# A two-block transformer kernel on one core: the start of the first FFN rebuilt, and three small jobs moved into the first mixer

## The chip, the cores and the metric

One Trainium2 chip (trn2), one NeuronCore of it. The metric is device time in microseconds (us) of one execution of the whole kernel, from its first instruction to its last and what lies around them; lower is better. A NeuronCore has five engines with queues of their own: TensorE (PE, matmuls, with weight loads shown as PEld), VectorE (DVE), ScalarE (ACT), GpSimd (POOL) and SyncE (SP, which issues the loads).

## The reference

Two transformer blocks on 256 tokens of width 1024, in float32. What matters here, cut from it:

```python
def first_block(x, ...):                       # 256 tokens x 1024
    h = h + 0.5 * swiglu(rmsnorm(h, ffn1_norm), ffn1_w_gate, ffn1_w_up, ffn1_w_down)   # FFN, hidden 2816
    n = rmsnorm(h, mix_norm); z = n @ w_in                                             # first mixer:
    ...  # attention, a spatial gate whose 8 weights of 128x128 (gmlp_w_s) are lower triangular
    h = h + merged @ w_out
    h = h + 0.5 * swiglu(rmsnorm(h, ffn2_norm), ffn2_w_gate, ffn2_w_up, ffn2_w_down)
    return rmsnorm(h, final_norm)

def second_block(x, meta_tokens, lb_logits, ...):
    h = concatenate([meta_tokens, x])          # 16 meta tokens ahead of the 256
    lower_bounds = cumsum(softmax(lb_logits))  # of the forget gates of its recurrent mixer
    ...  # recurrent mixer and latent attention, merged
    h = h + rms_norm((silu(gt) * up) @ w_ffn_out, ffn_post_g)                          # third FFN
```

## The kernel before

**Precision.** Every float32 operand of a projection is split into a high part (rounded to the fast float32 format `F32R`, by ACT: a copy) and a low part (value less high part, by DVE: a subtraction). A product is three matmuls (`products`, L1408 to L1410): high x low, low x high, high x high.

**Slabs.** The weights stream in as slabs of 1 MB (128 x 2048 numbers) through a ring of three (`RING`). For slab n: SP loads `stage`, when slab n-3 is split; ACT writes `w_hi` (`split_hi`, L1062), when PE has used slab n-3; DVE writes `w_lo` (`split_lo`, L1225); PE does 48 matmuls of 256 columns with it. All four engines run a program written out by hand in a fixed order, and wait on each other's semaphores alone.

**FFN.** Eleven pairs J of hidden chunks; each pair takes three slabs: gate, up, down. DVE scales the gate sums by the row factor (L1248), ACT takes the Silu (L1090), DVE scales the up sums (L1256), multiplies (L1260), ACT and DVE split the product (L1099, L1263), and the down slab adds it into PSUM banks 4 to 7 (`down_slab`). Order on PE: gate of J+1, up of J+1, down of J. On DVE and ACT the splits of slabs stand between these steps: split of slab 3, up of J = 0, split of slab 4, gate of J = 1, split of slab 5, up of J = 1, splits of slabs 6 and 7. On all three engines the pairs run in loops of two (`Fori`).

**The first FFN's start.** PE transposes the vectors and x (L1930, L1934) into PSUM. DVE copies x from there to `h` (L1349, `tokens_in`); ACT takes the high part of x times the norm's gain (L1072) and the squares (L1065) from `h`, DVE the low part (L1231). Slab 0 is split in two halves (L1133, L1355), slab 1 in two (L1137, L1374). POOL adds up the squares (L952, L956); PE sums them over the partitions inside slab 1, after 30 of its 48 matmuls (`late_mean`, L1515 to L1518), ACT takes the root (L1081), DVE the inverse (L1238).

**What else stands there.** After slab 1 PE transposes the spatial weights and the meta tokens (L1505, L1509, `spatial_weights_and_meta`). DVE, after the first gate scaling, computes the forget bounds (L1323 to L1326), copies the spatial weights (L1329) and prepares the meta tokens (L1333 to L1340): ten instructions. ACT computes an exponential for the bounds (L1145) with a table load around it. In each FFN ACT clears the banks 4 to 7 by one write of 128 x 2048 zeros (L1108, `y_zeroed`), so that every down matmul can accumulate.

**First mixer.** 26 slabs, written out. DVE evacuates projection i (L427, L431), then splits slab i+3. `scores(0)` on PE stands after projection 4 and uses banks 4 to 7.

Of the kernel before, what the change touches and what calls it, by code (L numbers as in the profile page):

```python
# [20 lines left out]
F32 = mybir.dt.float32  # L21
# [5 lines left out]
P = 128  # L27
# [79 lines left out]
y_bank y_zeroed gate_scaled silu_done up_scaled hidden hid_hi_done hid_lo_done evac  # L107
# [16 lines left out]
def program(nc, a, vec_d, id_d, tab_d, out):  # L124
    ctx = ExitStack()
    with ctx:
# [52 lines left out]
        meta_tok = view(2304, D)  # L179
# [99 lines left out]
        def mixer1_act(act, split_hi, input_hi):  # L279
# [22 lines left out]
            for i in range(26):  # L302
# [13 lines left out]
                if i == 5:  # L316
                    exps(0)
# [27 lines left out]
        def mixer1_dve(dve, split_lo, seq, input_lo, residual, inverse):  # L345
# [3 lines left out]
            def acc(i):  # L349
                k = 6 if i == 2 else 2 * (i % 2)  # L350
                return ps[:, k:k + 2, 0:SEQ]

# [70 lines left out]
            for i in range(26):  # L423
# [47 lines left out]
                if i < 22 and i != 20 or i == 25:  # L471
                    split_lo(n + i + 3)
                if i == 5:
# [466 lines left out]
        def _(pool):  # L940
# [31 lines left out]

            pool.wait_ge(s["ws_T"], 1)
# [5 lines left out]

            pool.wait_ge(s["mean_done"], 1)  # L980
            sum_squares(ssx, sq, "sq_done", 4)
# [51 lines left out]
        def _(act):  # L1033
# [49 lines left out]
            def ffn(f, lookahead=True):  # L1083
# [10 lines left out]
                def hidden(J, m, it=None, pf=True):  # L1094
# [5 lines left out]
                    if pf:  # L1100
# [27 lines left out]
            act.wait_ge(s["vec_ready"], 1)  # L1128
            for b in range(4):
                if b in (0, 2):  # L1130
                    act.wait_ge(s["slab0_in"] if b == 0 else slab_in[0], 16)
                    w = slice(SLAB // 4 * b, SLAB // 4 * b + SLAB // 2)
                    nc.scalar.activation(w_hi[:, 0, w], stage[:, 0, w], ACT.Copy).then_inc(s["hi0_ready" if b == 0 else "hi_ready"], 1)  # L1133
                input_hi(ffn_input(0)[0], vec[:, VEC["ffn1_norm"]:], 0, [b], late=b > 1)
# [65 lines left out]
        def _(dve):  # L1200
# [41 lines left out]
            def ffn(f, rstd_count, lookahead=True):  # L1242
                n, J0 = N_FFN[f], PAIRS * f
                g0 = 0 if f == 0 else 4

                def gate(J, m, it=None, first=False):
                    dve.wait_ge(s["slab_used"], up(m + 1, it))
                    nc.vector.tensor_tensor(pair(ga_s), ps[:, g0:g0 + 2, 0:SEQ] if first else pair(ps[:, J % 2, :]), bc2,  # L1248
# [744 lines left out]
```

## Time and profile before

| | before |
|---|---|
| device time, median of 3 runs | 1068.17 us (1066.13 to 1070.47) |
| the profiled execution | 1068.94 us, its span 1066.8 us |
| PE busy | 1041.7 us, 98% of the span |
| DVE busy | 698.5 us, 65% |
| ACT busy | 518.3 us, 49% |
| POOL busy | 91.1 us, 9% |
| chain that ended last | PE 86%, DVE 7%, ACT 4%, issue 3% |
| granted TensorE clock, mean | 0.990 |

The times in the rows further down count from the span's start; the profiled execution took 2.1 us more than its span. Matmuls are pipelined, so a busy PE says nothing of its pace: the pace is read from the distance of the starts.

### The profile page before, as it was taken

How to read it: one execution, taken by the hardware profiler on the slowest of the kernel's cores; microseconds unless marked ns; L12 is line 12 of the kernel's file. 1: busy time of each engine (PE TensorE's matmuls, PEld its weight loads, DVE VectorE, ACT ScalarE, POOL GpSimd, SP SyncE). 2: the span in 40 equal slices, each digit the busy share in tenths (PEclk: the TensorE clock that was granted, in tenths of full speed). 3: DMA queues.
4: the chain of work that ended last, by engine and by line, in shares of the span. 5: the costliest groups of instructions: out<-in, count | busy, mean ns of one | idle time of the engine just before them, and what ended most of it. 6: DMA issues, size and time to landing. Idle time of an engine off the chain costs nothing.

```text
span 1066.8 us, 20377 instructions
## 1 busy us (share of the span) xinstructions
PE 1041.7 (98%) x8847; PEld 1019.7 (96%) x8847; DVE 698.5 (65%) x705; ACT 518.3 (49%) x572; POOL 91.1 (9%) x90
## 2 busy tenths in 40 slices
PE   8999999999999999999989899999999989999997
PEld 8999999999999999999989798999999989999997
DVE  6765565766958666655689757686747666656652
ACT  6543443636655554444476456513355465444344
POOL 3000000100202200000024800100000030000001
PEclk9999999999999999999999999999999989999999
DMA  9666655465455466566446533333335444665541
GB/s 312 195 210 200 209 175 197 159 207 188 141 175 167 156 213 215 178 199 210 134 135 200 157 119 119 119 100 100 119 119 168 165 143 159 217 207 167 197 156 39
DMA packets 147192, 179.89 MB, mean 169 GB/s; under 512 B 3965, under 2 KB 134258, under 8 KB 147138
## 3 DMA queue, kind: packets, MB, share of 16 engines
q1 hardware_dynamic: 146464, 177.55, 51.3%
q0 software_dynamic: 400, 1.43, 0.4%
q8 instruction: 42, 0.69, 0.3%
q10 hardware_dynamic: 274, 0.13, 0.0%
q14 instruction: 12, 0.10, 0.0%
HBM read 178.05 MB, written 1.05 MB: 168 GB/s over the span
## 4 chain that ended last, share of the span: by engine, by line
PE 86%; DVE 7%; ACT 4%; issue 3%; DMA 1%; DVEq 0%; ACTq 0%; SPq 0%
PE ps L1408 26%; PE ps L1409 26%; PE ps L1410 26%; PE ps L1785 2%; ACT w_hi L1062 2%; DVE w_lo L1225 1%; DMA stage<-in_ffn_w_gate_dram 1%; PE ps L1750 0%; DVE ar L693 0%; ACT L1038 0%; PE ps L1748 0%; DVE rstd L1238 0%; PE ps L1826 0%; PE ps L1761 0%; DVE ar L1256 0%
## 5 line engine op out<-in xcount | busy, mean ns | idle before, releaser
L1225 DVE TENSOR_TENSOR w_lo<-stage,w_hi 128x2048 fp32r<-128x2048 f32 x164 | 378.4, 2311 | 194.9 <-ACT w_hi L1062 194.8
L1408 PE MATMUL ps<-x_hi,w_lo 128*128 128x256 f32 (+1 forms) x1480 | 418.6, 283 | 7.2 <-DVE x_lo L1231 2.6
L1409 PE MATMUL ps<-x_lo,w_hi 128*128 128x256 f32 (+1 forms) x1480 | 414.3, 280 | 0.0
L1410 PE MATMUL ps<-x_hi,w_hi 128*128 128x256 f32 (+1 forms) x1480 | 414.1, 280 | 0.0
L1062 ACT ACTIVATE w_hi<-stage 128x2048 fp32r<-128x2048 f32 x164 | 311.5, 1905 | 195.4 <-PE ps L1410 193.0
L1408 PE MATMUL ps<-a_hi,w_lo 128*128 128x256 f32 (+1 forms) x1112 | 310.7, 279 | 4.4 <-DVE a_lo L1231 2.3
L1409 PE MATMUL ps<-a_lo,w_hi 128*128 128x256 f32 (+1 forms) x1112 | 309.3, 278 | 0.0
L1410 PE MATMUL ps<-a_hi,w_hi 128*128 128x256 f32 (+1 forms) x1112 | 309.3, 278 | 0.0
L1408 PEld LDWEIGHTS ps<-x_hi,w_lo 128*128 128x128 f32 x1480 | 279.9, 189 | 14.2 <-issue 10.1
L1410 PEld LDWEIGHTS ps<-x_hi,w_hi 128*128 128x128 f32 x1480 | 280.8, 190 | 0.0
L1409 PEld LDWEIGHTS ps<-x_lo,w_hi 128*128 128x128 f32 x1480 | 280.0, 189 | 0.1
L1408 PEld LDWEIGHTS ps<-a_hi,w_lo 128*128 128x128 f32 x1112 | 210.3, 189 | 5.6 <-issue 3.6
L1410 PEld LDWEIGHTS ps<-a_hi,w_hi 128*128 128x128 f32 x1112 | 210.5, 189 | 0.0
L1409 PEld LDWEIGHTS ps<-a_lo,w_hi 128*128 128x128 f32 x1112 | 210.3, 189 | 0.1
L1090 ACT ACTIVATE ar<-ar 128x512 f32<-128x512 f32 x33 | 20.8, 630 | 115.3 <-DVE ar L1248 115.3
L952 POOL TENSOR_TENSOR ss<-sq 128x256 f32<-128x256 f32 x7 | 6.4, 921 | 718.6 <-ACT sq L1065 378.4
L1099 ACT ACTIVATE x_hi<-ar 128x512 fp32r<-128x512 f32 x22 | 13.9, 633 | 81.4 <-DVE ar L1260 81.4
L1248 DVE TENSOR_TENSOR ar<-ps,rstd 128x512 f32<-128x512 f32 x33 | 22.8, 690 | 27.4 <-PE ps L1410 27.3
L956 POOL TENSOR_TENSOR ss<-ss,sq 128x256 f32<-128x256 f32 x36 | 31.1, 865 | 33.1 <-ACT sq L1065 22.4
L1785 PE MATMUL ps<-ar 128*128 128x64 f32 (+1 forms) x256 | 29.6, 273 | 1.3 <-DVE ar L693 1.3
L1785 PEld LDWEIGHTS ps<-ar 128*128 128x128 f32 x256 | 29.2, 192 | 1.7 <-issue 1.7
L1099 ACT ACTIVATE a_hi<-ar 128x512 fp32r<-128x512 f32 x11 | 7.0, 633 | 42.0 <-DVE ar L1260 42.0
(296 smaller groups left out, 810.5 us busy)
## 6 DMA issues: line engine op xcount, KB each, us to landing
stage<-in_w_in_dram SPq DMA_DIRECT2D x36, 1024.0 KB, 5.3
stage<-in_ffn_w_up_dram SPq DMA_DIRECT2D x22, 1024.0 KB, 5.4
stage<-in_ffn_w_down_dram SPq DMA_DIRECT2D x22, 1024.0 KB, 4.9
stage<-in_w_ffn_in_dram SPq DMA_DIRECT2D x22, 1024.0 KB, 5.1
stage<-in_ffn_w_gate_dram SPq DMA_DIRECT2D x21, 1024.0 KB, 5.3
stage<-in_w_ffn_out_dram SPq DMA_DIRECT2D x11, 1024.0 KB, 4.9
stage<-in_w_gate_dram SPq DMA_DIRECT2D x8, 1024.0 KB, 5.3
stage<-in_w_out_dram SPq DMA_DIRECT2D x8, 1024.0 KB, 4.9
```

The costliest lines, as they stand in the source:

```text
L952: seq(nc.gpsimd.tensor_tensor(dst, src[:, 0, :], src[:, 1, :], ALU.add))
L956: last = nc.gpsimd.tensor_tensor(dst, dst, src[:, c, :], ALU.add)
L1062: nc.scalar.activation(o, i, ACT.Copy).then_inc(s["hi_ready"], 1)
L1090: nc.scalar.activation(ga_a, ga_s, ACT.Silu).then_inc(s["silu_done"], 1)
L1099: nc.scalar.activation(hidden_part(f, 0, J), pair(hid), ACT.Copy).then_inc(s["hid_hi_done"], 1)
L1225: nc.vector.tensor_tensor(o, i, b.bitcast(F32), ALU.subtract).then_inc(s["lo_ready"], 1)
L1248: nc.vector.tensor_tensor(pair(ga_s), ps[:, g0:g0 + 2, 0:SEQ] if first else pair(ps[:, J % 2, :]), bc2, ALU.mult).then_inc(s["gate_scaled" ...
L1408: nc.tensor.matmul(o, wl, xh, start=start, stop=False, skip_group_check=skip)
L1409: nc.tensor.matmul(o, wh, xl, start=False, stop=False, skip_group_check=skip)
L1410: return nc.tensor.matmul(o, wh, xh, start=False, stop=stop, skip_group_check=skip)
L1785: last = nc.tensor.matmul(o, k2[:, hd, X0 + P * t:X0 + P * t + P], q, start=True, stop=True)
```

## The change

Four things change. (1) At the start ACT and DVE split x straight from PSUM (`first_rows`), slab 0 is split in quarters, and the squares (from PSUM too) and the copies to `h` come after slab 1's splits; on DVE the split of slab 2 now stands ahead of four tiny operations on `lb` and `gfp`. (2) The transposes of spatial weights and meta tokens go to the first mixer, after its projection 3, the DVE work on them too; the forget bounds and their exponential go to projections 7 and 5 there. On POOL the mixer's sum of squares goes ahead of the loads that wait for the spatial transposes. (3) `y_zeroed` is gone: the first down matmul into each bank starts the accumulation instead, and PE's first two pairs after J0 are written out ahead of its loop in each FFN. (4) The first gate sums of the first FFN go to banks 2 and 3 and the up sums to bank 0, and PE's gate J = 1 no longer waits for the first gate scaling.

```diff
+        def first_rows(c):
+            return ps[:, 4 + c // 2, SEQ * (c % 2):SEQ * (c % 2) + SEQ]
...
# ACT, start
             for b in range(4):
+                act.wait_ge(s["x_T"], b + 1)
+                for c in (2 * b, 2 * b + 1):
+                    nc.scalar.activation(x_hi[:, c, X0:], first_rows(c), ACT.Copy, scale=g[:, c:c + 1]).then_inc(s["xhi_done"], 1)
                 if b in (0, 2):
                     act.wait_ge(s["slab0_in"] if b == 0 else slab_in[0], 16)
-                    w = slice(SLAB // 4 * b, SLAB // 4 * b + SLAB // 2)
-                input_hi(ffn_input(0)[0], vec[:, VEC["ffn1_norm"]:], 0, [b], late=b > 1)
+                w = slice(SLAB // 4 * b, SLAB // 4 * b + SLAB // 4)
+                nc.scalar.activation(w_hi[:, 0, w], stage[:, 0, w], ACT.Copy).then_inc(s["hi0_ready" if b < 3 else "hi_ready"], 1)
             wait_slab(act, 1, None)
             for c in range(2):
                 ...                                   # a half of slab 1
+                if c == 0:
+                    first_squares(0)
+                    first_squares(1)
-            squares(2)
-            squares(3)
+            first_squares(2)
+            first_squares(3)
             load_table(ACT.Sqrt)
             split_hi(2)
-            root(1, ps[:, 3, 0:SEQ], loaded=True)
-            act.wait_ge(s["lb_ready"], 1)
-            nc.scalar.activation(lb[:, 1:3, :], lb[:, 1:3, :], ACT.Exp).then_inc(s["lb_exp"], 1)
+            root(1, ps[:, 1, 0:SEQ], loaded=True)
             load_table(ACT.Silu)
...
# DVE, gate of an FFN
-                    if f == 0 and first:
-                        spatial_weights_and_meta()
                     split_lo(m + 3, it)
...
# DVE, start
+            for b in range(4):
+                for c in (2 * b, 2 * b + 1):
+                    dve.wait_ge(s["xhi_done"], 2 * b + 2)
+                    nc.vector.scalar_tensor_tensor(out=x_lo[:, c, X0:], in0=first_rows(c), scalar=g[:, c:c + 1],
+                                                   in1=x_hi[:, c, X0:].bitcast(F32), op0=ALU.mult,
+                                                   op1=ALU.subtract).then_inc(s["xlo_done"], 1)
+                dve.wait_ge(s["hi0_ready" if b < 3 else "hi_ready"], b + 1 if b < 3 else 1)
+                ...                                   # w_lo of that quarter
             for c in range(2):
                 ...                                   # the halves of slab 1
+            for b in range(4):
+                tokens_in(b)                          # waits for sq_done, b + 1
+            split_lo(2)
...
# ACT, FFN
-                act.wait_ge(s["meta_T_copied"], 1)
-                act.wait_ge(s["up_scaled"], J0 + 1)
-                nc.scalar.activation(ps[:, 4:8, :].rearrange("p b c -> p (b c)"), ones[:, 0:1].to_broadcast([P, 4 * 512]),
-                                     ACT.Copy, scale=0.0).then_inc(s["y_zeroed"], 1)
...
# PE, FFN
                 if f == 0:
                     gate(J0, n, first=True)
-                    second_slab(halves(2), ffn_input(f), lambda: late_mean(norm, "sq_done", ps[:, 3, 0:SEQ]))
-                    spatial_weights_and_meta()
+                    second_slab(halves(0), ffn_input(f), lambda: late_mean(norm, "sq_done", ps[:, 1, 0:SEQ]))
                     pe.wait_ge(s["std_ready"], rec)
-                    pe.wait_ge(s["gate_scaled"], J0 + 1)
...
-                with pe.Fori(0, (PAIRS - 1) // 2) as it:
+                for b in range(2):
+                    J = J0 + 1 + b
+                    gate(J, n + 2 + 3 * b)
+                    upward(J, n + 3 + 3 * b)
+                    down_slab(f, n + 4 + 3 * b, J - 1, first=b == 0)
+                with pe.Fori(0, (PAIRS - 3) // 2) as it:
...
# PE, first mixer
+                    if i == 3:
+                        spatial_weights_and_meta()
                     if i == 4:
                         pe.wait_ge(s["std_ready"], 3)
+                        pe.wait_ge(s["ws_T_copied"], 1)
+                        pe.wait_ge(s["meta_T_copied"], 1)
                         scores(0)
```

Two places of the order on DVE and one on PE show the moves. DVE before, from slab 1's split to the split of slab 3 (`lb`, `gfp`: bounds and a gain; `ar<-ps 128x1024`: the spatial weights; `meta`: the meta tokens):

```order
L1374 TENSOR_TENSOR w_lo<-stage,w_hi 128x8x128 x2
L1377 TENSOR_TENSOR lb<-vec 128x8
...
L1225 TENSOR_TENSOR w_lo<-stage,w_hi 128x2048
L1238 RECIPROCAL rstd<-std 128x256
L1248 TENSOR_TENSOR ar<-ps,rstd 128x512
L1323 TENSOR_TENSOR lb<-lb 128x8
...
L1329 COPY ar<-ps 128x1024
L1333 COPY meta<-ps 128x128
...
L1340 TENSOR_TENSOR x_lo<-meta,x_hi 128x8x16
L1225 TENSOR_TENSOR w_lo<-stage,w_hi 128x2048
```

DVE of the changed kernel, the same stretch:

```order
L1379 TENSOR_TENSOR w_lo<-stage,w_hi 128x8x128 x2
L1363 COPY h<-ps 128x512 x4
L1264 TENSOR_TENSOR w_lo<-stage,w_hi 128x2048
L1385 TENSOR_TENSOR lb<-vec 128x8
L1386 TENSOR_TENSOR lb<-vec,lb 128x8
L1387 TENSOR_TENSOR lb<-vec,lb 128x8
L1388 TENSOR_TENSOR gfp<-vec 128x8
L1277 RECIPROCAL rstd<-std 128x256
L1288 TENSOR_TENSOR ar<-ps,rstd 128x512
L1264 TENSOR_TENSOR w_lo<-stage,w_hi 128x2048
```

The split of slab 3 now follows the first gate scaling directly, the four copies to `h` stand behind slab 1, and the four tiny operations stand between the split of slab 2 and the inverse. PE of the changed kernel in the first mixer, at the end of projection 3 and the start of projection 4:

```order
L1417 MATMUL ps<-x_hi,w_hi 128x256
L1619 MATMUL ps<-ident,ar 128x128 x8
L1623 MATMUL ps<-ident,ar 128x16 x8
L1415 MATMUL ps<-w_hi,x_lo 128x256
L1416 MATMUL ps<-w_lo,x_hi 128x256
```

The sixteen transposes that stood between slab 1 and slab 2 of the first FFN stand there.

## Rows read from the trace of the kernel before

**Rows 1.** Page, busy time: us, share of the span, instructions.

```profile
PE 1041.7 (98%) x8847; PEld 1019.7 (96%) x8847; DVE 698.5 (65%) x705; ACT 518.3 (49%) x572; POOL 91.1 (9%) x90
```

**Rows 2.** Waits of the whole span, PE: us in total, times, longest.

```profile
PE ps L1408 <- DVE ar L1256: 0.3, 1, 0.3
```

**Rows 3.** Timeline, DVE: start us, us, line op, [idle before <- releaser].

```profile
20.39 2.39 DVE L1225 TENSOR_TENSOR w_lo<-stage,w_hi 128x2048 fp32r<-128x2048 f32 x1 [0.71 <-ACT w_hi L1062]
23.27 1.75 DVE L1238 RECIPROCAL rstd<-std 128x256 f32<-128x256 f32 x1 [0.49 <-ACT std L1081]
25.06 0.69 DVE L1248 TENSOR_TENSOR ar<-ps,rstd 128x512 f32<-128x512 f32 x1
25.67 0.16 DVE L1323 TENSOR_TENSOR lb<-lb 128x8 f32<-128x8 f32 x1
...
26.54 1.23 DVE L1329 COPY ar<-ps 128x1024 f32<-128x1024 f32 x1
...
29.41 2.29 DVE L1225 TENSOR_TENSOR w_lo<-stage,w_hi 128x2048 fp32r<-128x2048 f32 x1
...
47.13 4.49 DVE L1225 TENSOR_TENSOR w_lo<-stage,w_hi 128x2048 fp32r<-128x2048 f32 x2 [1.04 <-ACT w_hi L1062]
```

**Rows 4.** Timeline, PE, first and last matmuls of even stretches.

```profile
21.27 0.60 PE L1515 MATMUL ps<-ss,ones 128*128 128x256 f32 x2
...
22.68 0.28 PE L1409 MATMUL ps<-x_lo,w_hi 128*128 128x256 f32 x1
...
24.51 0.28 PE L1410 MATMUL ps<-x_hi,w_hi 128*128 128x256 f32 x1
24.62 1.04 PE L1505 MATMUL ps<-ident,ar 128*128 128x128 f32 x8
...
26.42 0.28 PE L1409 MATMUL ps<-x_lo,w_hi 128*128 128x256 f32 x1
...
31.84 0.28 PE L1410 MATMUL ps<-x_hi,w_hi 128*128 128x256 f32 x1
...
32.66 0.28 PE L1409 MATMUL ps<-x_lo,w_hi 128*128 128x256 f32 x1
...
49.39 0.28 PE L1410 MATMUL ps<-x_hi,w_hi 128*128 128x256 f32 x1
49.50 0.36 PE L1408 MATMUL ps<-x_hi,w_lo 128*128 128x256 f32 x1
...
196.37 0.28 PE L1410 MATMUL ps<-a_hi,w_hi 128*128 128x256 f32 x1
```

**Rows 5.** Timeline, ACT, in the first stage.

```profile
14.01 1.99 ACT L1137 ACTIVATE w_hi<-stage 128x1024 fp32r<-128x1024 f32 x2
15.90 1.14 ACT L1065 ACTIVATE sq<-h 128x512 f32<-128x512 f32 x2
...
23.26 1.28 ACT L1145 ACT_TABLE_LOAD   x1
...
26.19 1.90 ACT L1062 ACTIVATE w_hi<-stage 128x2048 fp32r<-128x2048 f32 x1
```

**Rows 6.** DMA, slab 1 alone, issued at 3.03: KB, us from issue to landing.

```profile
stage<-in_ffn_w_up_dram SPq DMA_DIRECT2D x1, 1024.0 KB, 9.6
```

**Rows 7.** Timeline, POOL: pairs of additions of squares, at two places.

```profile
16.66 2.93 POOL L956 TENSOR_TENSOR ss<-ss,sq 128x256 f32<-128x256 f32 x2 [3.51 <-ACT sq L1065]
...
199.84 1.55 POOL L956 TENSOR_TENSOR ss<-ss,sq 128x256 f32<-128x256 f32 x2 [1.40 <-ACT sq L1065]
```

**Rows 8.** Timeline, second FFN: PE, and ACT clearing the banks.

```profile
377.51 0.38 PE L1408 MATMUL ps<-x_hi,w_lo 128*128 128x256 f32 x1 [0.15 <-DVE w_lo L1225]
...
389.05 0.38 PE L1408 MATMUL ps<-a_hi,w_lo 128*128 128x256 f32 x1 [0.37 <-DVE w_lo L1225]
...
374.96 1.86 ACT L1108 ACTIVATE ps<-ones 128x2048 f32<-128x2048 f32 x1
```

**Rows 9.** Timeline, DVE, first mixer: the evacuation of projection 4.

```profile
225.78 0.88 DVE L431 TENSOR_SCALAR ar<-ps,rcol 128x256 f32<-128x256 f32 x2 [1.14 <-PE ps L1410]
```

More of the change, by code:

```diff
@@ L106 @@
 h_new xhi_done xlo_done sq_done ss_ready mean_done std_ready rstd_ready
-y_bank y_zeroed gate_scaled silu_done up_scaled hidden hid_hi_done hid_lo_done evac
+y_bank gate_scaled silu_done up_scaled hidden hid_hi_done hid_lo_done evac
 hT_T hT_copied yg_done ysq_done yg_T out_copied
@@ L316, in mixer1_act @@
                 if i == 5:
+                    act.wait_ge(s["lb_ready"], 1)
+                    nc.scalar.activation(lb[:, 1:3, :], lb[:, 1:3, :], ACT.Exp).then_inc(s["lb_exp"], 1)
                     exps(0)
@@ L1255, in hidden @@
                     dve.wait_ge(s["slab_used"], up(m + 1, it))
-                    nc.vector.tensor_tensor(pair(up_s), ps[:, 6:8, 0:SEQ] if first else pair(ps[:, 2 + J % 2, :]), bc2,
+                    nc.vector.tensor_tensor(pair(up_s), first_up if first else pair(ps[:, 2 + J % 2, :]), bc2,
                                             ALU.mult).then_inc(s["up_scaled"], 1)
@@ L1270, in ffn @@
                 gate(J0, n, first=True)
-                hidden(J0, n + 1, first=f > 0)
+                hidden(J0, n + 1, first=True)
                 loops = (PAIRS - 1) // 2 if lookahead else (PAIRS - 3) // 2
@@ L1423, in feature_slab @@
                     for k in range(DC):
-                        if n == 0 and k == 4:
+                        if n == 0 and k in (2, 4):
+                            pe.wait_ge(s["lo0_ready"], k // 2 + 1)
+                        if n == 0 and k == 6:
                             slab_ready(n)
@@ L1470, in first_slabs, with down_slab @@
                 part(1, (DC - 2, DC - 1)).then_inc(s["slab_used"], 1)
-            def down_slab(f, n, J, last_one=False, it=None):
+            def down_slab(f, n, J, last_one=False, it=None, first=False):
                 slab_ready(n, it)
@@ L1481, in down_slab @@
                     last = products(o, wh[:, k, P * m:P * m + P], wl[:, k, P * m:P * m + P], hh[:, k, :], hl[:, k, :],
-                                    False, last_one and k == 1, skip=True)
+                                    first and k == 0 and m % 2 == 0, last_one and k == 1, skip=True)
                     if last_one and k == 1 and m in (1, 3, 5):
@@ L1500, in turn @@
                     last.then_inc(s[done], 1)
-            def spatial_weights_and_meta():
-                pe.wait_ge(s["ws_masked"], 1)
-                for g in range(GG):
-                    last = nc.tensor.transpose(ps[:, 4 + g // 4, P * (g % 4):P * (g % 4) + P], ws[:, g, :], ident[:])
-                last.then_inc(s["ws_T"], 1)
-                pe.wait_ge(s["meta_loaded"], 16)
-                for c in range(DC):
-                    last = nc.tensor.transpose(ps[:, 6, META * c:META * c + META], meta_tok[0:META, P * c:P * c + P], ident[0:META, 0:META])
-                last.then_inc(s["meta_T"], 1)
             def late_mean(k, squares_done, o):
@@ L1604, in scores, with spatial_weights_and_meta @@
                     last.then_inc(s["s1_mm"], 1)
+                def spatial_weights_and_meta():
+                    pe.wait_ge(s["evac"], 3)
+                    pe.wait_ge(s["ws_masked"], 1)
+                    for g in range(GG):
+                        last = nc.tensor.transpose(ps[:, 6 + g // 4, P * (g % 4):P * (g % 4) + P], ws[:, g, :], ident[:])
+                    last.then_inc(s["ws_T"], 1)
+                    pe.wait_ge(s["meta_loaded"], 16)
+                    for c in range(DC):
+                        last = nc.tensor.transpose(ps[:, 5, META * c:META * c + META], meta_tok[0:META, P * c:P * c + P], ident[0:META, 0:META])
+                    last.then_inc(s["meta_T"], 1)
                 def turn_probs(g):
```

103 lines of the change are left out of this document (51 added, 52 removed).

## The prediction

> **What bounds the kernel now.** I read the page first: PE is busy for 98% of the span [rows 1], so what counts is when each slab starts on PE and how far apart its matmuls start. Then the waits: in the whole first FFN after slab 1 PE is recorded as waiting once, 0.3 us for the scaled up sums [rows 2]. So removing waits of PE by name can bring little. Then PE's timeline, by distances of starts [rows 4], which shows three things.
>
> First, slab 2 does not follow slab 1: the last matmul of slab 1 starts at 24.51, the second of slab 2 at 26.42, with sixteen transposes between. Against two ordinary steps of 0.113 that is 1.91 - 0.23 = 1.68 us of PE.
>
> Second, matmuls of one form run at two paces. From 32.66 to 49.39 there are 142 steps: 16.73 / 142 = 0.1178 us. From 49.50 to 196.37 there are 1295 steps (27 slabs of 48 matmuls): 146.87 / 1295 = 0.1134. A pace, once taken, stays until PE stands still for a moment: after the transposes it is the slow one (26.42 to 31.84, 46 steps, 0.1178), after the mean's matmuls the fast one (22.68 to 24.51, 16 steps, 0.1144), and the first FFN's whole loop from slab 6 on, entered after a short stand, is fast. I call them slow and fast pace; why the engine takes one I cannot tell from this trace.
>
> Third, slab 6 (first at 49.50) is handed over by DVE: its low part is the first of the two splits at 47.13, done at 47.13 + 4.49 / 2 = 49.38 [rows 3], 0.1 ahead of PE. So up to slab 6 PE runs just behind a chain of DVE and ACT: inverse (23.27), gate scaling (25.06), ten instructions for bounds, spatial weights and meta tokens (25.67 to 29.41), split of slab 3 (29.41), and so on to 49.38. From the start of split 3 to the end of split 6 it takes 49.38 - 29.41 = 19.97. In the second FFN PE waits for the same splits, 0.15 us at slab 4 and 0.37 at slab 6 [rows 8]: at the fast pace this chain is the slower one by a little.
>
> **The change part by part.**
>
> *The inverse.* ACT now has slab 1 as its first obstacle: issued at 3.03, landing 9.6 later [rows 6], at 12.6. The split of its halves took 15.90 - 14.01 = 1.89, two squares 1.14, and from the end of the squares (17.04) to the start of DVE's split 2 (20.39) it was 3.35 [rows 3, 5]. With four squares now: 12.65 + 1.89 + 2 x 1.14 + 3.35 = 20.2 for split 2 on DVE, so 0.2 earlier. It ends at 22.5 (2.3 long), the four tiny operations now behind it cost about what the four like them took between 25.67 and 26.54, 0.87 [rows 3], and the inverse starts at 23.4 against 23.27. So the whole rebuilding of the start gains nothing on DVE's chain, and I book +0.1.
>
> *The ten DVE instructions.* Gone from the chain: 29.41 - 25.67 = 3.74. Split 3 could start at 25.67 + 0.1 = 25.8. Its high part must be there: ACT's split of slab 3 began at 26.19, 4.92 after the mean (21.27), with the table load of 1.28 and the exponential itself (about 0.25 with its start) ahead of it [rows 4, 5]. Without them: 3.4 after the mean M, 1.9 long, so M + 5.3. With M = 20.1 (next item) that is 25.4: in time. Then split 6 ends at 25.8 + 19.97 = 45.8.
>
> *PE up to slab 6.* In the old kernel slab 0 ended near 21.27 - 30 x 0.118 - 0.1 = 17.6. Now ACT has no squares ahead of slab 1 and is through with slab 0 about when slab 1 lands, 12.6; DVE's last quarter follows about 1 later, and twelve matmuls hang on it: PE can't end slab 0 before 13.6 + 12 x 0.118 = 15.0, and at worst ends it as before, 17.6. Between these I take 16.5. M is then 16.5 + 3.6 = 20.1, if the sum of squares is there. POOL starts its five additions when the first squares are done, one half of slab 1 (0.95) and one square (0.57) after 12.65, about 14.2. A pair of additions took 2.93 beside DVE's splits and 1.55 elsewhere [rows 7]: five take 3.9 to 7.3, so 18.1 to 21.5. I take 19.2, since from 17 to 20 DVE only copies from PSUM. M lies in 18.7 to 21.5. Slab 2 follows slab 1 now, at M + 3.35 (24.62 - 21.27) = 23.45; its bank, its split (22.5) and the four copies are free by then. Four slabs at the fast pace (the one after the mean, 48 x 0.1134 = 5.44 each) bring PE to slab 6 at 45.2, before the split (45.8). So DVE's chain decides, slab 6 starts at 45.85 instead of 49.50: **-3.65**. With M = 21.5 it would be 46.6, 0.75 less.
>
> By the Trainium skill (SBUF — State Buffer, Who interferes with whom) a DVE instruction with two SBUF inputs shuts GpSimd's reads out, one with a single SBUF input does not. The two pairs above agree (2.93 beside splits, 1.55 without); by this rule alone the additions would be near 19 us, with the low parts of x now read from PSUM.
>
> *The moved transposes.* PE does them between projections 3 and 4 of the first mixer, where it had no gap: **+1.68**. After transposes the pace was slow, so I book it for the one slab up to `scores(0)`: 48 x 0.0044 = **+0.2**. DVE's part, 3.74 less the bounds' 0.87 = 2.87, falls into its idle time: the evacuation at 225.78 waited 1.14 for PE [rows 9], and PE comes 1.9 later now, so 3.0 are free. If the cover were gone, the scores would wait for the copied weights, at most 2 us. On POOL the four loads for the spatial gate are issued about 195 us later than before, behind that transpose, and the mixer's sum of squares was put ahead of them; nothing queues behind them until the layer norm some 40 us on. Forget bounds and exponential (0.87 and 0.25) fall among DVE's and ACT's slack there; 0.
>
> *Zeroing.* ACT's write of 1.86 in the second FFN starts at 374.96, ends at 376.82, and PE's down slab starts at 377.51, waiting for the split [rows 8]: hidden. 0 in all three FFNs. PE's written-out pairs do the same matmuls; 0.
>
> The Trainium skill (Runtime: NRT & Kernel Launch, Instruction fetch mechanics) says that a taken branch out of the fetched window stalls the engine, by which fewer passes of PE's loops would save a stall in each FFN. Four back-edges lie between 49.50 and 196.37 and the mean step there is 0.1134 with all of them in it; no run here shows such a stall, and I book nothing.
>
> *Sum.* -3.65 + 1.68 + 0.2 = -1.8. The profiled execution took 1068.94, so 1067.2 on its scale; it lies 0.8 above the median of the runs, 1068.17, so 1066.4 on the median's.
>
> **The rivals.**
>
> *A, the likeliest (0.55):* the sum, 1066.4, with its own range of 1064.4 to 1068.4 (the runs of before spread over 4.3 us).
>
> *B, slower: the first FFN keeps the slow pace (0.14).* The old kernel got out of it by its short stand at slab 6. If slab 2 starts at the slow pace now, PE reaches slab 6 at 23.45 + 4 x 5.65 = 46.05, after the split (45.8): no stand, and the loop of 27 slabs stays slow, 1295 x 0.0044 = +5.7. Time: 1066.4 + 0.2 + 5.7 = 1072.3. It decides at slab 2: slow there, and slab 6 ready. Against it: the mean left the fast pace, and the transposes which led to the slow one are gone. The same may hit another FFN's loop, 5.7 more (0.04).
>
> *C, nothing comes of it (0.13):* the DVE chain starts later than I think (the tiny operations and copies in the way, the sum of squares at 21.5 and more), or DVE is late in the mixer. Each 1 us of delay of the inverse costs 1 us, and 2 us make it 1068.2.
>
> *D, faster (0.14):* the shift lets other slow stretches of the mixers turn fast. Some 16 slabs more are 16 x 48 x 0.0044 = 3.4: 1063.0. A new stand of the clock could add to it.
>
> **Numbers.** What a measurement of this kernel can tell from no change is about 0.5%, 5.3 us: below 1062.8 or above 1073.5. From D about half and a little of A: 0.11 faster. From B with a second loop, and from B by the runs' spread: 0.10 slower. The rest, 0.79, lies within. The range from 1063.0 to 1072.5 takes in C and most of D and B.
>
> **What would show it.** Right: inverse near 23.4, split 3 directly behind the gate scaling at about 25.8, first matmul of slab 6 at 45.9, and steps of 0.113 from slab 2 on; sixteen transposes at about 216 in the mixer with slow steps behind them; the second and third FFN as before. Wrong: the mean's matmuls waiting for POOL beyond 20.6; slow steps through the first FFN (then B); a wait of PE for the copied spatial weights; a gap at the start of a loop.

## The result and the profile after

| | before | after |
|---|---|---|
| median of 15 executions each, us | 1070.47 | 1076.63 |
| lowest and highest, us | 1065.43 to 1078.41 | 1071.55 to 1084.96 |
| executions below 1069.5 us | 7 of 15 | 0 of 15 |
| profiled execution: span / time, us | 1066.8 / 1068.94 | 1073.6 / 1075.36 |

The ratio is 1.0068 with a 95% interval of 1.0046 to 1.009: slower, where the prediction had 1066.4, a range up to 1072.5 and a chance of 0.10 for slower. Here and below a ratio leaves out executions that lie over 1.5% above the fastest of their kernel, and a mean keeps them.

The first FFN did nearly what was forecast. DVE's timeline of the kernel after (start us, duration us, line and operation), to be laid beside [rows 3]:

```profile
20.89 2.93 DVE L1264 TENSOR_TENSOR w_lo<-stage,w_hi 128x2048 fp32r<-128x2048 f32 x1
...
24.29 1.75 DVE L1277 RECIPROCAL rstd<-std 128x256 f32<-128x256 f32 x1
26.07 0.69 DVE L1288 TENSOR_TENSOR ar<-ps,rstd 128x512 f32<-128x512 f32 x1
26.68 2.28 DVE L1264 TENSOR_TENSOR w_lo<-stage,w_hi 128x2048 fp32r<-128x2048 f32 x1
...
44.42 4.49 DVE L1264 TENSOR_TENSOR w_lo<-stage,w_hi 128x2048 fp32r<-128x2048 f32 x2 [1.04 <-ACT w_hi L1097]
```

The split of slab 3 starts at 26.68 instead of 29.41, directly behind the gate scaling, and the split of slab 6 ends at 44.42 + 4.49 / 2 = 46.67 instead of 49.38. PE's timeline of the same kernel, to be laid beside [rows 4 and 8]: the mean, the stand at slab 6, the end of the first FFN, the moved transposes, and slabs 4 and 6 of the second FFN. (A stand of PE is a step from one start to the next that is longer than an ordinary one. Where a length is given for it, it is the whole step, with the ordinary 0.11 us in it.)

```profile
20.69 0.70 PE L1516 MATMUL ps<-ss,ones 128*128 128x256 f32 x2
...
46.26 0.28 PE L1417 MATMUL ps<-x_hi,w_hi 128*128 128x256 f32 x1
46.85 0.36 PE L1415 MATMUL ps<-x_hi,w_lo 128*128 128x256 f32 x1 [0.32 <-DVE w_lo L1264]
...
193.71 0.28 PE L1417 MATMUL ps<-a_hi,w_hi 128*128 128x256 f32 x1
...
217.37 0.28 PE L1417 MATMUL ps<-x_hi,w_hi 128*128 128x256 f32 x1
217.49 1.04 PE L1619 MATMUL ps<-ident,ar 128*128 128x128 f32 x8
218.45 0.67 PE L1623 MATMUL ps<-ident,ar 16*128 16x16 f32 x8
219.05 0.39 PE L1415 MATMUL ps<-w_hi,x_lo 128*128 128x256 f32 x1
219.27 0.28 PE L1416 MATMUL ps<-w_lo,x_hi 128*128 128x256 f32 x1
...
378.48 0.39 PE L1415 MATMUL ps<-x_hi,w_lo 128*128 128x256 f32 x1
...
389.39 0.28 PE L1417 MATMUL ps<-a_hi,w_hi 128*128 128x256 f32 x1
390.17 0.36 PE L1415 MATMUL ps<-a_hi,w_lo 128*128 128x256 f32 x1 [0.51 <-DVE w_lo L1264]
```

Slab 6 comes at 46.85 instead of 49.50 and the first FFN ends at 193.71 instead of 196.37: 2.66 gained. The transposes cost 219.27 - 217.37 - 2 x 0.113 = 1.67 in the mixer, measured as the prediction did it. Behind them the kernel is still 1 us ahead. It loses that, and another 1 us, to slow stretches up to the second FFN (between 340 and 363 us PE does 198 matmuls, 205 in the kernel before, at a granted clock of 1.00 in both), and comes to slab 4 of the second FFN at 378.48, where the kernel before came at 377.51. Then PE stands 0.78 us at slab 6 of the second FFN, and what follows, the far larger loss, is seen in the view by stretches, here 130 us out of the loop of each FFN (busy us, matmuls in it, granted clock, DMA share, GB/s). The kernel before:

```profile
60.00:190.00 130.00, 130.00 (x1149) 1.00 0.61 198
400.00:530.00 130.00, 130.00 (x1149) 1.00 0.59 191
920.00:1050.00 130.00, 130.00 (x1150) 1.00 0.51 170
```

and the kernel after:

```profile
60.00:190.00 130.00, 130.00 (x1150) 1.00 0.60 194
400.00:530.00 130.00, 130.00 (x1106) 1.00 0.59 192
920.00:1050.00 130.00, 130.00 (x1149) 1.00 0.55 184
```

PE counts as 100% busy in all six, at a granted clock of 1.00 (the 2.4 GHz level), and yet one of them holds 1106 matmuls where the others hold 1149 or 1150. That is the slow pace: 130 / 1106 = 0.1175 us against 130 / 1149.5 = 0.1131. Over the 1295 steps of a loop it is 1295 x 0.0044 = 5.7 us. It lasts for the whole loop, and the number of matmuls in a window shows it best. Of the 6.8 us between the two spans it is 5.7.

### The profile page after: what moved, and what is told of

The parts are those of the page before. It is cut to its first block, busy times and chain, and to the rows that moved or that the text cites. A ratio compares the mean times of both kernels' runs of the same rounds, so it can differ in the third digit from the quotient of the medians.

```text
span 1073.6 us, 20360 instructions
## 1 busy us (share of the span) xinstructions
PE 1048.6 (98%) x8847; PEld 1026.1 (96%) x8847; DVE 698.6 (65%) x707; ACT 511.6 (48%) x570; POOL 91.1 (8%) x90
## 4 chain that ended last, share of the span: by engine, by line
PE 83%; DVE 7%; ACT 5%; issue 3%; DMA 1%; SPq 0%; DVEq 0%; ACTq 0%
PE ps L1415 26%; PE ps L1416 25%; PE ps L1417 25%; ACT w_hi L1097 3%; PE ps L1809 2%; DVE w_lo L1264 2%; DMA stage<-in_ffn_w_up_dram 1%; ACT L1073 1%; PE ps L1774 0%; DVE ar L728 0%; DVE ar L1298 0%; DVE ar L1294 0%; PE ps L1772 0%; DVE rstd L1277 0%; PE ps L1850 0%
## 5 line engine op out<-in xcount | busy, mean ns | idle before, releaser
L1301 DVE TENSOR_TENSOR x_lo<-ar,x_hi 128x512 fp32r<-128x512 f32 x22 | 15.2, 692 | 17.6 <-ACT x_hi L1134 17.6
```

Source lines behind the costliest of these rows:

```text
L1301: nc.vector.tensor_tensor(hidden_part(f, 1, J), pair(hid), hidden_part(f, 0, J).bitcast(F32), ALU.subtract).then_inc(s["hid_lo_done"], 1)
```

## The experiments

All executions of a kernel and of the kernel before it stand side by side on one chip; means are over all executions (the profiled one too), except for one of 1152 and one of 1156 us, which are left out. The sets stand on several chips, so each kernel is best compared with the mean of before beside it: 1070.6 for after, 1070.8 for loops_back and one_fp32, 1068.6 for after_more, before_written_out and loop_from_pair2, 1069.9 for before_ffn1_out, pair2_again, ffn1_from_pair2 and ffn23_from_pair2, 1071.5 for the two hi_first kernels and before_late6, 1070.9 for pad4 and combo. "Slow" is the FFN whose loop holds 1106 or 1107 matmuls in its window of the profiled execution; in all others it is 1149 or 1150.

| kernel | executions | mean, us | below 1069.5 | slow in the profile | span, us |
|---|---|---|---|---|---|
| before (beside after) | 15 | 1070.6 | 7 | none | 1066.8 |
| before_again | 1 | 1067.1 | 1 | none | 1064.9 |
| after | 15 | 1076.8 | 0 | second | 1073.6 |
| after_again | 1 | 1073.0 | 0 | first | 1071.3 |
| after_more | 11 | 1076.1 | 0 | first | 1070.0 |
| loops_back | 12 | 1072.5 | 3 | third | 1071.3 |
| one_fp32 | 12 | 1073.9 | 1 | first | 1071.8 |
| before_written_out | 12 | 1073.3 | 3 | first | 1072.3 |
| before_ffn1_out | 12 | 1071.8 | 4 | none | 1066.9 |
| loop_from_pair2 | 12 | 1072.3 | 2 | none | 1063.7 |
| pair2_again | 11 | 1072.4 | 3 | third | 1070.0 |
| ffn1_from_pair2 | 12 | 1072.2 | 2 | second, third | 1073.4 |
| ffn23_from_pair2 | 12 | 1072.7 | 1 | third | 1069.8 |
| hi_first6 | 12 | 1072.5 | 2 | third | 1068.5 |
| hi_first46 | 12 | 1076.1 | 2 | first, second | 1075.9 |
| before_late6 | 12 | 1074.5 | 1 | third | 1070.9 |
| pad4 | 12 | 1075.2 | 1 | second, third | 1077.4 |
| combo | 12 | 1067.3 | 9 | none | 1064.0 |
| combo_again | 12 | 1068.5 | 8 | first | 1069.7 |

The last two columns belong together: no slow loop 1063.7 to 1066.9, one 1068.5 to 1073.6, two 1073.4 to 1077.4. For what is left over the traces show two sources. The mixers have slow stretches too. And in ten of the 19 profiles in this table the granted clock falls to 0.5 (the 1.2 GHz level) for 3.4 us somewhere between 607 and 624 us, which makes the same 1000 matmuls around it last 131.6 to 131.8 us instead of 130.1 to 130.3; before and after have it, before_again, after_again and after_more do not. Over 598 to 628 us the granted clock is 0.94 in the first two and 1.00 in the other three.

**The same two kernels again** (no edit).

> The kernel before, profiled once more. Theory (the paces are set by the program at each stand of PE): the steps between matmul starts come out as in the first profile, fast (0.1134 us) in all three FFN loops, last matmul of the second FFN near 536. Rival (the pace is drawn anew at each stand of PE, whatever the program): some FFN loop of the three comes out at 0.1177 us, or a mixer stretch changes its pace, and the span changes by 5.7 us for each loop.

> The changed kernel, profiled once more. Theory (paces set by the program): the second FFN's loop is slow again (0.1177 us per step from about 390 to 543), the other two fast, span within 1 us of 1073.6. Rival (drawn anew at each stand): the second FFN's loop comes out fast with some chance, and the span is then near 1067.8, or another loop comes out slow.

> The changed kernel again, profiled and timed beside the kernel before on this chip. Theory (a draw for each FFN loop, about 1.6 of three slow): median 1074 to 1078, times in steps of about 5.8 us, the slow loops not the same ones as in the other two profiles of it. Rival (fixed by the program): the second FFN's loop is slow as in the first profile.

before_again: 1067.08 us, all loops fast. after_again, 1073.05 us, and after_more have the slow loop elsewhere. The stretches of after_again:

```profile
60.00:190.00 130.00, 130.00 (x1107) 1.00 0.56 188
400.00:530.00 130.00, 130.00 (x1150) 1.00 0.59 199
920.00:1050.00 130.00, 130.00 (x1150) 1.00 0.52 178
```

The same program, and now the first FFN is slow and the second fast. So the pace isn't fixed by the program: it differs between executions, as if drawn in each. after_more, ratio 1.0076 (1.0043 to 1.0108), confirms the loss: with the first two sets 0 of 27 executions of after lie below 1069.5. Less their one slow loop of 5.7 us, the spans of the three profiles of after would be 1067.9, 1065.6 and 1064.3, in the mean 1065.9; before has 1066.8 and 1064.9, in the mean 1065.8. These profiles show no gain that is left without the slow loops.

**Which form PE's code has at the stands.** The change writes out the first two pairs of each FFN on PE, so that the stands at slab 4 and slab 6 no longer fall inside a loop. loops_back gives the second and third FFN their old loop and zeroing back (all code from here on is shortened):

```
-for b in range(2): gate, upward, down_slab(first=b == 0)     # f > 0
-with pe.Fori(0, (PAIRS - 3) // 2) as it: ...
+with pe.Fori(0, (PAIRS - 1) // 2) as it: ... pe.wait_ge(s["y_zeroed"], f)
```

> After, but in the second and third FFN PE's loop of five passes and ACT's zeroing of the y banks are as before; the first FFN keeps the written-out pairs. Theory (the second FFN's loop at the slow pace is what made the change slower, and the written-out pairs with the start flag put it there): that loop is fast again, 5.8 us are gone, 1070.8 on the scale where after has 1076.6. Rival (the slow pace comes from what is earlier, when the stands fall, and not from the loop's form): still slow, 1076.6. Rival (drawn anew at each stand): either, with no connection to the edit.

Ratio to before 1.0017 (0.9982 to 1.0052); mean 1072.5, 3.6 to 4.3 below the two larger sets of after. Some two thirds of what was expected, but the one profile has its slow loop in the third FFN, in loop code: the written-out pairs aren't the only way into it.

The other way round, before_written_out puts written-out pairs into the old kernel and nothing else, before_ffn1_out only in the first FFN:

```
-with pe.Fori(0, (PAIRS - 1) // 2) as it:       # in before: all pairs
+for b in range(2): gate(J, ...); upward(J, ...); pe.wait_ge(s["y_zeroed"], f + 1); down_slab(...)
+with pe.Fori(0, (PAIRS - 3) // 2) as it:       # from the third pair on
```

> Before, with the first two pairs of each FFN written out on PE in front of the loop, as after has them; nothing else (the zeroing, the transposes and the start stay as before). Theory (at the short stand at slab 6 of an FFN the pace is drawn, and code that is written out there draws the slow one more often, about 1.6 of three loops where the loop's own code gives 0.6): 5 to 6 us more in the mean of many executions, 1075 to 1076 against 1070, and the lowest times rare. Rival (the form of PE's loop has nothing to do with it): 1070, within 0.3%.

> Before, with the first two pairs written out in the first FFN alone. Theory: 3 to 4 us more than before, as much as with all three written out (1072 to 1074 in the mean), the first FFN's loop slow in the profile. Rival (the form of the code is not the cause): as before, mean 1069 to 1071.

Ratios 1.0036 (1.0005 to 1.0066) and 1.0028 (1.0005 to 1.0051). The same matmuls and the same waits, written out, cost the old kernel time: 4.7 us in the mean against the executions of before on its side (1068.6, the lowest of its six sets), and 1.9 for the first FFN alone (1069.9). The first is slower than the rival said and faster than the theory. The second lies between the two as well, and the slow loop that the theory wanted in its profile is not there.

loop_from_pair2 keeps the first pair written out and starts the loop with the second, so that slab 4 stays written out and slab 6 is in the loop; the next two do it in the first FFN alone and in the other two alone:

```
+one_pair(1)                                      # written out, start flag
+with pe.Fori(0, (PAIRS - 3) // 2) as it: for b in range(2): one_pair(2 + b, it)
+one_pair(PAIRS - 1)
```

> After, with PE's loop begun one pair earlier in all three FFNs, so that the stand at slab 6 falls inside the loop again (its last pair is written out instead); no zeroing, start flag, start and transposes as in after. Theory (written-out code at the stand draws the slow pace more often): 1069 to 1070 in the median where after has 1076, single runs down to 1065. Rival (something else in the change does it, such as the moved transposes or the length of the stand): 1073 to 1077 as after.

> The kernel with PE's loop begun at the second pair in all three FFNs once more, for more executions of it and a second profile. Theory: first FFN's loop fast again; median 1070 to 1072. Rival (its fast profile was chance): a slow loop in the profile, median 1073 or more.

> After, with PE's loop begun at the second pair in the first FFN alone; the second and third FFN as in after. In the profiles so far the first FFN's loop was slow in 4 of 6 kernels where its first pairs are written out, and in none of 3 where the stand at slab 6 falls inside the loop. Theory (the first FFN's loop is what the written-out pairs spoil): its loop is fast, and the median falls by 3 to 4 us, to 1072 to 1073. Rival (the draws are spread evenly over the FFNs or have another cause): 1075 to 1077.

> The complement: PE's loop begun at the second pair in the second and third FFN, the first FFN as in after. Theory (the first FFN is what counts): little gained, 1074 to 1076, the first FFN's loop slow in the profile. Rival (each FFN's written-out pairs cost the same): 1072 to 1073.

Ratios 1.0034 (1.0006 to 1.0063), 1.0014 (0.9977 to 1.005), 1.0025 (1.0 to 1.0049) and 1.0034 (1.0008 to 1.0059). All four lie near 1072.4, some 4 us below after and above what the theory had for the first two (pair2_again has a slow loop in its profile besides); whether the first FFN, the other two or all three are moved makes no difference that can be told. ffn1_from_pair2 alone came out as its theory had it; ffn23_from_pair2 came out as its rival had it, and with that the theory that the first FFN alone counts has fallen.

**What runs, and how long PE stands.** one_fp32 adds one fp32 matmul like the mean's behind the wait of slab 6:

```
+if it is None and m == n + 6:
+    slab_ready(m)
+    nc.tensor.matmul(halves(2 + J % 2)[0], ones[:], ss[:, 0, X0:], start=True, stop=True)
```

> After, plus one fp32 matmul of 256 columns (ones by the sums of squares, as in the mean) into the free bank at the start of slab n+6 of each FFN, its result overwritten. Theory (fp32 matmuls such as the mean's, with the wait around them, put PE at the fast pace): the second FFN's loop is at 0.1134 us, 5.8 us less one matmul of about 0.9 in each FFN: 1072 to 1073.5 on the scale where after has 1076.6. Rival (the pace doesn't depend on what ran last): loop slow, 1077 to 1079.

1.0024 (0.9993 to 1.0055), but the first FFN's loop is slow right behind such a matmul, so it doesn't set the fast pace. That it has fewer slow executions than after I can't explain by it.

late_before cuts each split in 32 DVE instructions, so that DVE is late. PE does not stand at most slabs, as was expected, but at about every second (13 stands of over 0.3 us between 56 and 240 us, some 27 slabs), and then for up to 2.8 us:

```
+for q in range(31):
+    nc.vector.tensor_tensor(o[:, w * q:w * q + w], i[:, w * q:w * q + w], b[...], ALU.subtract)
```

> Before, with each low-part split cut into 32 DVE instructions, so that DVE is late and PE stands at most slabs. Theory (each stand draws the pace anew, and between stands it stays): slabs behind a stand come out fast or slow, mixed, never another pace within a slab. Rival (the pace is a property of the place in the program or of the buffers): the same slab of each pass shows the same pace. Time: some 1.5 us more per slab, 1150 to 1250.

1287.76 us; part of it is the clock, since behind the longer stands the matmuls run for 3.4 us at 0.215 us per step, at a granted clock of 0.50 (163 to 165 us). Four stretches of 13 us in the first FFN, each between two such stands and behind the clock's return:

```profile
104.00:117.00 13.00, 13.00 (x116) 0.99 0.53 177
125.00:138.00 13.00, 13.00 (x117) 1.00 0.49 162
145.00:158.00 13.00, 13.00 (x116) 1.00 0.51 163
166.00:179.00 13.00, 13.00 (x112) 1.00 0.46 161
```

Three are fast, the fourth is slow, and it is the same place in the loop as the second, one pass (40 us) later. Within the stretches the pace stays, between them it changes in both directions. That fits the theory's draw, within a single execution; stand and fall of the clock come together here, so it doesn't say which of the two changes the pace.

hi_first6 does the 16 matmuls of slab 6 that need only the high part ahead of the wait for the low part; hi_first46 does the same in slab 4:

```
+pe.wait_ge(s["hi_ready"], n + 1)
+for k in range(DC): matmul(outs[0], wh, x_hi, start=k == 0); matmul(outs[0], wh, x_lo)
+slab_ready(n)
+for k in range(DC): matmul(outs[0], wl, x_hi)
```

> After, but in slab 6 of each FFN PE first does the 16 matmuls of its first half that read only the high part of the weights (ready some 1.5 us earlier), and waits for the low part behind them. Theory (the long stand at slab 6 is what draws the slow pace in about 4 of 10 cases): no stand at slab 6, the pace in which PE arrives is kept, mostly fast; 0.65 us less in each FFN by the stand itself and about one slow loop less: median 1066 to 1069 where after has 1076. Rival (the form of the code or something else draws the pace): 1073 to 1075, only the 2 us of the stands gained.

> As before it, and the same order in the first down slab (slab 4) of each FFN, where PE stands 0.35 us. Theory: one stand less in each FFN, another 0.3 us each; whatever pace PE takes after the mean stays for the whole FFN. Median 1065 to 1069. Rival: 1072 to 1075.

In the timeline of hi_first6 the stand is gone:

```profile
45.59 0.28 PE L1417 MATMUL ps<-x_hi,w_hi 128*128 128x256 f32 x1
45.70 0.28 PE L1452 MATMUL ps<-x_hi,w_hi 128*128 128x256 f32 x1
...
47.40 0.28 PE L1453 MATMUL ps<-x_lo,w_hi 128*128 128x256 f32 x1
47.51 1.07 PE L1456 MATMUL ps<-x_hi,w_lo 128*128 128x256 f32 x8
48.42 0.28 PE L1415 MATMUL ps<-x_hi,w_lo 128*128 128x256 f32 x1
```

Without a stand the pace is kept, as the theory said: the first two FFNs arrive fast and stay fast, the third arrives slow and stays slow. But the median is 1071.2, not the 1066 to 1069 expected (ratio 0.9988, 0.9955 to 1.0021, without two executions at 1081 and 1083; with them the mean is 1.0 above before). That a slow pace from ahead of slab 6 no longer recovers there would explain it, and the third FFN is a case. hi_first46, 1.0055 (1.0021 to 1.0089), is no better than after: in the second FFN PE stands 0.4 us one slab earlier instead, at 387.87, and leaves it slow. Both expectations failed in the time.

before_late6 and pad4 lengthen a stand without touching PE's code, in before at slab 6 (split in four instructions) and in after at slab 4 of the last two FFNs (split in two):

```
+split_lo(m + 3, it, pieces=4)                    # before_late6: slab 6 + 6 k
+split_lo(m + 3, it, pieces=2 if first and f > 0 else 1)   # pad4
```

> Before, with the split of slab 6 (and of each sixth slab after it, where DVE has time) cut into four DVE instructions, so that it ends about 0.5 us later and the stand at slab 6 is 0.7 to 1.1 us. Theory (long stands draw the slow pace more often than short ones): 1.5 us by the delay itself and about half a slow loop more on average, mean near 1074 where before has 1070. Rival (the length of the stand doesn't matter): 1071 to 1072.

> After, with DVE's split of slab 4 of the second and third FFN cut in two instructions, which ends it some 0.07 us later; PE's code is untouched. Theory (the length of the stand at slab 4 sets the pace behind it): PE stands 0.42 us there, goes slow for slabs 4 and 5, stands only about 0.2 us at slab 6 and leaves it fast in both FFNs; mean 1073 to 1074 where after has 1076.5. Rival (the form of the code sets it, or nothing that can be steered): fast behind slab 4, 0.7 us at slab 6, mean 1076.

before_late6: 1.0032 (1.0001 to 1.0063), mean 3.0 above the 1071.5 beside it, some 0.7 of it by the stands themselves (0.95, 0.44 and 0.44 us in its profile, 0.73, 0.24 and 0.20 in before_again); too close to both expectations to tell. pad4: 1.0031 (0.9995 to 1.0066), mean 1075.2, nearer to the rival's 1076 than to the theory's 1073 to 1074. Its timeline at slab 4 and slab 6 of the second FFN:

```profile
376.51 0.28 PE L1421 MATMUL ps<-a_hi,w_hi 128*128 128x256 f32 x1
...
376.93 0.39 PE L1419 MATMUL ps<-x_hi,w_lo 128*128 128x256 f32 x1
...
387.84 0.28 PE L1421 MATMUL ps<-a_hi,w_hi 128*128 128x256 f32 x1
388.51 0.37 SPq L900 DMA_DIRECT2D stage<-in_ffn_w_up_dram  x1
388.63 0.36 PE L1419 MATMUL ps<-a_hi,w_lo 128*128 128x256 f32 x1 [0.52 <-DVE w_lo L1268]
```

The stand at slab 4 is 0.42, as in loop code, and PE remains fast behind it (376.93 to 387.84), stands 0.8 at slab 6 and leaves it slow, in the second and the third FFN alike. So a stand of 0.42 us at slab 4 doesn't force the slow pace, as that theory had it. These are two draws, and they don't show that the length has no part in the odds; the counts over all profiles, below, leave room for it.

**The new start with the old loop.** combo is after, with PE's loop and the zeroing as in before in the second and third FFN, and the loop from the second pair on in the first (where the start flag is needed):

```
+lead = 1 if f == 0 else 0
+if lead: one_pair(1)
+with pe.Fori(0, (PAIRS - 1) // 2 - lead) as it: for b in range(2): one_pair(1 + lead + b, it)
+if lead: one_pair(PAIRS - 1)
```

> After with the new start and the moved transposes, but PE's loop as before with zeroing in the second and third FFN, and begun at the second pair in the first. Theory (written-out pairs at slabs 4 and 6 are what makes slow loops more frequent): as few slow loops as in before, on a base 1.5 us lower: mean 1068 to 1070, median 1067 to 1069, and so equal to or better than before. Rival (the rest of the change takes part): mean 1072.

> The same kernel a second time, for 12 more executions and a second profile. The same is expected: mean 1068 to 1070 by the theory, 1072 by the rival.

0.996 (0.9928 to 0.9992) and 0.9978 (0.9944 to 1.0011), medians 1066.09 and 1067.69 beside 1071.18 of before. 17 of 24 executions lie below 1069.5, against 0 of 27 of after. The second set came out where the theory had it, the first a little lower still (mean 1067.3 for 1068 to 1070). Against after this is clear; against before only the first set is clear of 1. The stretches of combo:

```profile
60.00:190.00 130.00, 130.00 (x1150) 1.00 0.61 194
400.00:530.00 130.00, 130.00 (x1150) 1.00 0.59 188
920.00:1050.00 130.00, 130.00 (x1150) 1.00 0.51 169
```

At slab 6 of its third FFN (903.01 + 4.49 / 2 = 905.25 is the end of the split) PE stands nearly as long as in the written-out kernels, but comes back sooner:

```profile
903.01 4.49 DVE L1268 TENSOR_TENSOR w_lo<-stage,w_hi 128x2048 fp32r<-128x2048 f32 x2 [1.05 <-ACT w_hi L1097]
...
904.71 0.28 PE L1421 MATMUL ps<-a_hi,w_hi 128*128 128x256 f32 x1
905.35 0.38 PE L1419 MATMUL ps<-a_hi,w_lo 128*128 128x256 f32 x1 [0.37 <-DVE w_lo L1268]
```

Here 0.10 us lie between the end of the split and the matmul; in after, at 390.17, it is 390.17 - (387.74 + 4.49 / 2) = 0.19. DVE's row for that one, and the split of slab 4 in the same kernel:

```profile
376.13 2.29 DVE L1264 TENSOR_TENSOR w_lo<-stage,w_hi 128x2048 fp32r<-128x2048 f32 x1 [1.05 <-ACT w_hi L1097]
...
387.74 4.49 DVE L1264 TENSOR_TENSOR w_lo<-stage,w_hi 128x2048 fp32r<-128x2048 f32 x2 [1.05 <-ACT w_hi L1097]
```

At slab 4 of the second FFN it is the other way round: 378.48 - (376.13 + 2.29) = 0.06 written out, and 0.13 in loop code (377.51 less the end of the split, 377.38, in before).

**Over all profiles.** Where the wait at slab 6 is written out, 9 of 23 FFN loops came out slow (hi_first6 and hi_first46, which don't wait there, not counted); where it is in loop code, 5 of 28; where the loop begins with the first pair, 2 of 17. By these counts alone the difference isn't shown: 9 of 23 against 5 of 28 or further apart comes of chance about once in eight times. What shows it are the times, 17 of 24 executions below 1069.5 against 0 of 27 (combo's two sets and the three of after).

The same 51 loops can be sorted by what PE does ahead of them, and that gives another reading. Behind a stand of over 0.7 us at slab 6, 9 of 23 came out slow; behind a shorter one or none, 5 of 28. The length depends on the pace at which PE arrives: 0.64 us and more whenever it arrives fast, 0.60 and less whenever it arrives slow. And that pace is often taken at slab 4. In the second and third FFN, where PE reached slab 4 fast, it left it slow in 7 of 12 cases with the wait in loop code (0.43 us), and in 1 of 16 with the wait written out (0.36, in pad4 0.42). Of those seven loops six then came out fast. So the old loop may be saved by a slow slab 4, which shortens the stand at slab 6. No kernel here separates this from the form of the code at slab 6.

## Why the prediction was wrong

*The inverse* (+0.1 forecast): 24.29 instead of 23.4, so +1.0. DVE's split 2 started 0.7 later than I had it, right behind the copies to `h`, and took 2.93 instead of 2.3, its first part beside POOL's work. POOL's timeline:

```profile
15.21 1.29 POOL L987 TENSOR_TENSOR ss<-sq 128x256 f32<-128x256 f32 x1 [13.91 <-ACT sq L1163]
16.58 4.05 POOL L991 TENSOR_TENSOR ss<-ss,sq 128x256 f32<-128x256 f32 x4
20.59 1.09 POOL L1004 TENSOR_SCALAR_AFFINE_SELECT ar<-ar 128x1024 f32<-128x1024 f32 x1
```

The five additions took 5.42 from 15.21, within my 3.9 to 7.3, and the mean came at 20.69, within 18.7 to 21.5. The Trainium skill (SBUF — State Buffer, Who interferes with whom) says that a DVE instruction with two SBUF inputs contends with a GpSimd instruction that reads SBUF. The trace agrees: the split that began at 20.89, with 0.79 us of POOL's select (20.59 to 21.68) beside it, was 0.6 us longer than the 2.29 of a lone one [rows 3].

*The ten DVE instructions* (-3.74): right. Split 3 lies directly behind the gate scaling, and from its start to the end of split 6 it is 46.67 - 26.68 = 19.99, forecast 19.97.

*PE up to slab 6* (-3.65): right in kind, -2.65, smaller by the 0.9 of the inverse; DVE's chain decides, as said, and PE waits for it. In after_again and after_more slab 6 comes at 46.46 and 46.43, in before_again at 49.06: -2.6 there as well.

*The moved transposes* (+1.68 and +0.2): 1.67, as forecast, and slow steps behind them up to the scores. But from the end of the first FFN to slab 4 of the second it took 181.1 us in before and in before_again, and 184.8, 184.3 and 183.2 in the three profiles of after: +2.1 to +3.7 instead of +1.88. The rest went in slow stretches on the way there, mostly of the first mixer, which I had left as they were. (Rival D had them turn fast.)

*The sum* of -1.8 is not shown, even where no loop goes slow. The start gave 2.6 to 2.7, and the mixer took 2.1 and more. The three profiles of after, less their slow loop, come to the same mean as the two of before. Two related kernels without a slow loop have 1063.7 and 1064.0 against 1064.9 and 1066.8, so some gain is possible.

**The step that failed** is the one I gave a price of zero, "PE's written-out pairs do the same matmuls; 0", together with the reading that carried it: "the first FFN's whole loop from slab 6 on, entered after a short stand, is fast". I had forecast the stand at slab 6 myself (PE at 45.2, the split at 45.8), and took from one profile that PE leaves it fast. It is a draw of 5.7 us per FFN: all three profiles of after have one slow loop, the two of before have none. By the means, some 1076.5 against some 1070, I estimate 6.5 / 5.7, about 1.1 slow loops more per execution, of three, if all of the difference is in the loops.

*Rival B* had the right mechanism and price (a whole loop slow, 5.7 each), but too narrow a condition: I had it come when PE reaches slab 6 slow and without a stand. That happened once, in combo_again, and in five other first FFNs that came so the loop went fast. More often the slow pace came behind a long stand, in any FFN. So 0.14, and 0.04 for a second one, were far too low, and the range ended 4 us short of the median. That the three times of before lay 4.3 us apart was in view; I took it for noise, where some of it may have been the same draw (the profiled execution of the three had no slow loop; the others aren't known).

*Loops against written-out code.* By the Trainium skill (Runtime: NRT & Kernel Launch, Instruction fetch mechanics) taken branches can stall and unrolling is preferred. In no loop here did such a stall show (1149 matmuls in 130 us with the back-edges in them), and the kernels with more code written out were the slower ones, by 4.7 us in before_written_out.

**What stays open:** why the form of the code changes the odds. combo against after and, more weakly, before_written_out against before show that it does. The 0.19 against 0.10 us between release and first matmul is a difference that goes with it at slab 6; at slab 4 the signs are reversed, and neither is shown to be the cause. The length of the stand at slab 6, which slab 4 helps to set, is as good a candidate. The zeroing and the start flag were moved together with the loops in loops_back and combo, but before_written_out keeps the zeroing and loses time all the same. The mixers have stands and paces of their own, worth some 2 us up to the second FFN in the first profile of after; what the change does to them wasn't tested apart.

## What to carry to other kernels

Count the matmuls in equal windows of even stretches before pricing microseconds: PE at 100% busy and full clock can still run 4% slower for 150 us. Where single executions differ by more than the change is to bring, take several profiles first and ask whether the spread comes of draws (here of 5.7 us each); then a change must be judged by its share of bad draws as well. An edit that only rewrites how an engine's code is laid out, at a place where this engine stands and resumes, isn't free: make it apart from the rest and time it with a dozen executions; here the kernel with the new start and the old loop is some 8.5 us faster in the mean than the one as changed, and 3.0 faster than the one before, the latter just clear of noise in one set of two.

## What the hardware showed unexpectedly

Pairs of weight load and matmul of 256 columns have two stable spacings at the same granted clock of 1.00: 0.1131 and 0.1175 us. The Trainium skill (TensorE: Matmul & The Clock Gate, Back-to-back issue gap) gives a single sustained spacing for such pairs at each of two sizes (81 ns at 128 columns, 131 ns at 512) and tells nothing of a second one. A pace is kept over loops of 147 us with all their back-edges, and nearly every change has a stand of PE ahead of it, if only a step 0.04 us longer than an ordinary one. Twice none is to be seen, both times at the start of slab 5 of the first FFN (at 40.7 in the profile of after, at 40.3 in that of after_more, each with a step of 0.12 us). A stand of one length can be followed by either pace (0.43 us at slab 4 in loop code: 7 slow, 5 fast), and so can an fp32 matmul run just before (one_fp32: one loop slow, two fast). Whether the length shifts the odds is open.
